# Seven block products in place of eight in the second feed-forward product of a streaming encoder step

## What is computed

```python
hn = rmsnorm(x, norm2_g[l]) * (1 + sc2) + sh2
x = x + gt2 * (jnp.square(jax.nn.relu(hn @ w_ff1[l])) @ w_ff2[l])
...
y = rmsnorm(x, final_norm_g) * (1 + scf) + shf
```

## Time and profile before

| what | value |
|---|---|
| median of three executions | 1235.04 us |
| the profiled execution, its own time | 1234.25 us |
| its span, first to last instruction | 1232.4 us |
| PE busy | 1208.6 us, 98% of the span |
| DVE, ACT, POOL busy | 722.8, 440.6 and 120.7 us |
| granted clock of PE, mean of the span | 0.994 |

### The profile page before, as it was taken

How to read it: one execution, slowest core, us unless ns; L and a number is a source line. 1 busy time by engine, 2 the same in 40 slices (tenths; PEclk the granted TensorE clock), 3 DMA queues, 4 the chain that set the end, 5 groups by cost and what they waited for, 6 DMA issues and landing times.

```text
span 1232.4 us, 25278 instructions
## 1 busy us (share of the span) xinstructions
PE 1208.6 (98%) x10327; PEld 1156.4 (94%) x10327; DVE 722.8 (59%) x1087; ACT 440.6 (36%) x768; POOL 120.7 (10%) x282
## 2 busy tenths in 40 slices
PE   6999999999999999999999999999999999999997
PEld 3899999989999999999999999969999999999997
DVE  5686776545565564544968995574643444444445
ACT  4584443123232222324343333363332332233254
POOL 4111112102002021021110001000300000000000
PEclk8999999999999999999999999999999999999999
DMA  9722323222222122135864567422422322222212
GB/s 328 243 79 77 86 72 93 62 53 70 62 69 79 51 71 58 40 108 157 240 202 127 164 214 282 147 61 77 135 86 85 86 86 82 85 80 79 87 54 77
DMA packets 181559, 135.32 MB, mean 110 GB/s; under 512 B 4554, under 2 KB 168876, under 8 KB 180184
## 3 DMA queue, kind: packets, MB, share of 16 engines
q1 hardware_dynamic: 174228, 105.36, 29.2%
q0 software_dynamic: 6976, 28.48, 6.9%
q10 hardware_dynamic: 260, 0.10, 0.0%
HBM read 128.02 MB, written 5.90 MB: 109 GB/s over the span
## 4 chain that ended last, share of the span: by engine, by line
PE 94%; DVE 3%; ACT 1%; DMA 1%; SPq 1%; issue 1%; POOL 0%; DVEq 0%; ACTq 0%
PE gp L625 17%; PE gp L626 16%; PE gp L627 16%; PE gp L630 12%; PE gp L629 12%; PE gp L618 9%; PE dp L865 2%; PE dp L875 1%; DMA ada_w<-in_ada_w 1%; PE dp L932 1%; PE dp L898 1%; PE dp L925 1%; PE dp L917 1%; PE dp L877 1%; PE dp L904 1%; PE dp L835 1%
## 5 line engine op out<-in xcount | busy, mean ns | idle before, releaser
L625 PE MATMUL gp<-a_pair,w_hi 128*128 128x384 f32 x832 | 290.6, 349 | 3.9 <-DVE w_lo L1518 2.3
L626 PE MATMUL gp<-a_pair,w_hi 128*128 128x384 f32 x832 | 280.5, 337 | 0.0
L627 PE MATMUL gp<-a_pair,w_hi 128*128 128x384 f32 x832 | 279.7, 336 | 0.0
L630 PE MATMUL gp<-a_pair,w_lo 128*128 128x288 f32 x832 | 245.5, 295 | 0.0
L629 PE MATMUL gp<-a_pair,w_lo 128*128 128x288 f32 x832 | 243.8, 293 | 0.0
L1518 DVE TENSOR_TENSOR w_lo<-w_raw,w_hi 128x1024 fp32r<-128x1024 f32 x160 | 197.9, 1237 | 54.9 <-ACT w_hi L1117 54.7
L1271 ACT ACTIVATE xp<-gp 128x576 f32<-128x576 f32 x113 | 73.6, 652 | 419.1 <-PE gp L630 391.6
L1530 DVE TENSOR_TENSOR xp<-xp,gp 128x288 f32<-128x288 f32 x95 | 43.0, 453 | 226.2 <-ACT xp L1271 225.7
L625 PEld LDWEIGHTS gp<-a_pair,w_hi 128*128 128x128 f32 x832 | 156.1, 188 | 15.8 <-issue 6.2
L1117 ACT ACTIVATE w_hi<-w_raw 128x1024 fp32r<-128x1024 f32 x160 | 168.5, 1053 | 0.0
L626 PEld LDWEIGHTS gp<-a_pair,w_hi 128*128 128x128 f32 x832 | 156.7, 188 | 0.2 <-issue 0.2
(11 more groups left out here) (333 smaller groups left out, 1709.7 us busy)
## 6 DMA issues: line engine op xcount, KB each, us to landing
w_raw<-in_w_in SPq DMA_DIRECT2D x72, 512.0 KB, 3.9
w_raw<-in_w_ff SPq DMA_DIRECT2D x64, 512.0 KB, 4.1
ada_half<-in_ada_w POOLq DMA_DIRECT2D x32, 512.0 KB, 4.7
ada_w<-in_ada_w SPq DMA_DIRECT2D x16, 512.0 KB, 9.9
w_raw<-in_w_a_out SPq DMA_DIRECT2D x8, 512.0 KB, 4.8
w_raw<-in_w_b_out SPq DMA_DIRECT2D x8, 512.0 KB, 4.6
w_raw<-in_w_o SPq DMA_DIRECT2D x8, 512.0 KB, 6.5
fin_vu<-in_final_ada_w POOLq DMA_DIRECT2D x4, 1024.0 KB, 18.5
```

Of the source, the lines that this page charges most:

```text
L625: T_.matmul(front, w_hi[:, b, k, :], hi[:, 0:CUT], start=first, stop=False)
L626: T_.matmul(front, w_hi[:, b, k, :], lo[:, 0:CUT], start=False, stop=last)
L627: T_.matmul(both.rearrange("p (e c) -> p e c", e=2)[:, :, REST // 2:HALF], w_hi[:, b, k, :], pair[:, :, k, CUT:T], start=first, stop=last)
L630: return T_.matmul(back[:, REST:REST + HALF], w_lo[:, b, k, :], hi[:, HALF:T], start=False, stop=last, skip_group_check=True)
```

## The change

In quarters 0, 1 and 2, `ff2` is done on pairs of output tiles. A pair is a product of 2 x 2 blocks: two output tiles, two halves of the quarter's 1024 rows, two halves of 288 tokens. Eight block products become seven, of sums and differences of blocks (the scheme that is known by Strassen's and Winograd's names). Quarter 3 keeps its eight tiles.

- A block product is 4 steps of 3 matmuls of 288 columns. PE does seven of them for a pair (`seven_products`), on sums that accumulate in three PSUM banks. ACT copies the running sum out after the products 0, 1, 2 and 6 (`snapshot`), and DVE adds the products 3, 4 and 5 to those copies (`z_add`). PE waits for a copy before it goes on adding to the same bank.
- DVE makes four sums of weight blocks for each pair (`op_sums`). Rounded parts come from ACT (`op_hi`, four instructions a pair), rests from DVE (`op_lo`, four a pair), and `op_ready` counts the rests. Those of a quarter's first pair are made during the last four hidden tiles.
- Each two hidden tiles become eight blocks of 288 tokens, four as they are and four differences (`f_sum`), each rounded and split (`f_hi`, `f_hi_late`, `f_lo`). Tiles t and t + 4 stand side by side, so the order of the hidden tiles is 0, 4, 1, 5, 2, 6, 3, 7.
- There is one set of blocks `fo` in place of two buffers, and the order is ff1(0), ff2(0), ff1(1), ff2(1), ff1(2), ff2(2), ff1(3), ff2(3).
- `z_tok`, `shift` and `final_b` move to the place of `a_pair`, so POOL loads `final_b` and `shift` only when the last hidden tile is done. `ff1` and `ff2` are written out in place of loops.

```diff
+PRODUCTS = ((4, R11), (5, T1), (6, T2), (0, R22), (1, T3), (2, R21), (3, T4))
+BANK_C, BANK_A = 1, 3
...
         pool.wait_ge(S["ada_used"], 3 * KT)
+        pool.wait_ge(S["tile_done"], ordinal(N_FF + 55) + 1)
         pool.dma_start(final_b[:, :], A["final_ada_b"][0:D].rearrange("(o d) -> o d", o=1).to_broadcast([P, D]))\
...
+        def seven_products(q, m):
...
+            for at, (slot, op) in enumerate(PRODUCTS):
+                pe.wait_ge(S["op_ready"], 4 * i + (1, 2, 2, 3, 3, 4, 4)[at])
...
+                elif at == 1:
+                    if m:
+                        pe.wait_ge(S["z_added"], 3 * i - 2)
+                elif at == 2:
+                    pe.wait_ge(S["snapped"], 4 * i + 1)
+                elif at == 3:
+                    pe.wait_ge(S["snapped"], 4 * i + 2)
...
+                for k in range(KH):
+                    if m == 0:
+                        pe.wait_ge(S["f_split"], 12 * q + 3 * k + (1 if op in (R11, T1) else 3 if op in (T3, T4) else 2))
+                    T_.matmul(out, hi[:, k, :], fo[:, 0, k, op, :], start=(opens and k == 0), stop=False,
+                              skip_group_check=not opens)
+                    T_.matmul(out, hi[:, k, :], fo[:, 1, k, op, :], start=False, stop=False, skip_group_check=not opens)
+                    last = T_.matmul(out, lo[:, k, :], fo[:, 0, k, op, :], start=False, stop=(k == KH - 1),
+                                     skip_group_check=not opens)
+                last.then_inc(S["part_done"], 1)
...
         for q in range(3):
-            group8(N_FF + 8 + 16 * q, a_pair)
+            for m in range(4):
+                seven_products(q, m)
...
+            products(n, 0, a_pair, summed=kept(n) + 1)
...
+        def ff1(q):
+            for t in range(KT):
+                n, b = N_FF + 16 * q + t, t % 2
+                evac(n, b, xp[:, b, 0:T], also="tmp_free", value=n - N_WA + 1)
+                if q == 0 and t == 0:
+                    act.wait_ge(S["ada_used"], 3 * KT)
+                if t < 6 or q == 3:
+                    w_next(n + 2)
+                f_hi(q, t)
+                if q < 3:
+                    if b:
+                        f_hi_late(q, t)
+                    if t >= 4:
+                        op_hi(q, 0, t - 4)
...
+        def ff2(q):
...
+                snapshot(i, 0, chain, xp[:, 0, 0:HALF])
+                if m < 3:
+                    op_hi(q, m + 1, 0)
+                act.wait_ge(S["tmp_free"], n - N_WA + 2)
+                snapshot(i, 1, more, xp[:, 1, HALF:T])
+                snapshot(i, 2, chain, xp[:, 0, HALF:T])
...
-        ff1(0, N_FF)
+        ff1(0)
         ada_rows(B2, mrow_l, 3 * KT, 3)
         for q in range(3):
-            ff1(q + 1, N_FF + 8 + 16 * q)
-            ff2(q, N_FF + 16 + 16 * q)
+            ff2(q)
+            ff1(q + 1)
...
+                elif b == 0:
+                    f_sum(T1, R12, R11, "tmp_free", squared).then_inc(S["f_raw"], 1)
+                    if t < 6:
+                        lo_split(n + 2, (n + 2) % 4)
+                    dve.wait_ge(S["f_hi_done"], 12 * q + 3 * u + 1)
+                    f_lo(q, t, R11, T1 + 1, 2)
...
+                    elif t == 6:
+                        op_lo(q, 0, 1)
+                        op_sums(q, 0, 1)
+                        op_sums(q, 0, 2)
+                        op_lo(q, 0, 2)
...
+                z_add(i, 5, alone, xp[:, 0, 0:HALF])
+                if m == 3:
+                    lo_split(n + 2, (n + 2) % 4)
+                dve.wait_ge(S["z_added"], 3 * i + 3)
+                add_residual(2 * m, 0).then_inc(S["tmp_free"], 1)
+                if m < 3:
+                    op_lo(q, m + 1, 1)
...
```

More of the change, by code:

```diff
@@ L53, with ordinal, pair_of, kept @@
 PLAIN = N_WA - N_TAIL
+KH = KT // 2
+R11, R12, T1, R21, R22, T2, T3, T4 = range(8)
+NOP = 8
+TILE_ORDER = (0, 4, 1, 5, 2, 6, 3, 7)
+PRODUCTS = ((4, R11), (5, T1), (6, T2), (0, R22), (1, T3), (2, R21), (3, T4))
+BANK_C, BANK_A = 1, 3
+def ordinal(n):
+    return n - 8 * min((n - N_FF) // 16, 3) if n >= N_FF else n
+def pair_of(q, m):
+    return 4 * q + m
+def kept(n):
+    return ordinal(n) - PLAIN
 RAW, SLOT = 4, 2
@@ L399, in _, with ff_load @@
         group8(N_WO, w_o)
[L400 to L404, removed]
+        def ff_load(n, w, col, row=0):
+            before = n - 4
+            q, r = divmod(before - N_FF, 16)
+            if before >= N_FF and r >= 8 and q < 3:
+                sp.wait_ge(S["op_ready"], 4 * (pair_of(q, (r - 8) // 2) + 1))
+            else:
+                sp.wait_ge(S["w_lo_done"], ordinal(before) + 1)
+            sp.dma_start(w_raw[:, n % 4, :, :], wt(w, col, row)).then_inc(raw_full[n % 4], 16)
+        for q in range(4):
+            for t in range(KT):
+                at = TILE_ORDER[t] if q < 3 else t
+                ff_load(N_FF + 16 * q + t, w_ff1, q * D + at * P)
+            for t in range(KT):
+                ff_load(N_FF + 16 * q + 8 + t, w_ff2, t * P, q * KT)
         for t in range(4):
@@ L627, in add_in @@
             T_.matmul(both.rearrange("p (e c) -> p e c", e=2)[:, :, REST // 2:HALF], w_hi[:, b, k, :],
-                      pair[:, :, k, CUT:T], start=first, stop=last)
+                      both_halves[:, :, CUT:T], start=first, stop=last)
             T_.matmul(front[:, 0:HALF], w_lo[:, b, k, :], hi[:, 0:HALF], start=False, stop=last, skip_group_check=True)
@@ L1087, in _ @@
         for n in range(N_ALL - KT, N_ALL - 1):
[L1088 removed]
+            products(n, n % 2, fo, "f_split", 36, summed=kept(n) + 1)
             f = n - N_ALL + KT - 1
@@ L1431, in _ @@
             modulated(1, 1, KT, f)
[L1433 to L1447, removed]
@@ new lines, in snapshot @@
+        def snapshot(i, at, bank, out):
+            act.wait_ge(S["part_done"], 7 * i + at + 1)
+            AC(out, bank, ACT.Copy).then_inc(S["snapped"], 1)
+        def ff2(q):
+            for m in range(4):
+                i, n = pair_of(q, m), N_FF + 16 * q + 8 + 2 * m
+                chain, more = gp[:, 2 * (m % 2), 0:HALF], gp[:, BANK_C, 0:HALF]
+                act.wait_ge(S["tmp_free"], n - N_WA + 1)
+                snapshot(i, 0, chain, xp[:, 0, 0:HALF])
[5 more added lines that the diff above has]
+                if m < 3:
+                    op_hi(q, m + 1, 1)
+                else:
+                    act.wait_ge(S["part_done"], 7 * i + 5)
+                    w_next(n + 2)
+                if m < 3:
+                    op_hi(q, m + 1, 2)
+                snapshot(i, 6, chain, xp[:, 1, 0:HALF])
+                if m < 3:
+                    op_hi(q, m + 1, 3)
+                else:
+                    w_next(n + 3)
@@ L1464, in _ @@
             if n + 2 < N_ALL:
-                free(n, n // 4, n % 4)
+                w_next(n + 2)
             if t == 0:
@@ L1992, in _ @@
         norm(rstd2, 1)
[L1994 to L2003 removed]
+        slot_lo = w_lo[:, :, :, :].rearrange("p b (h k) n -> p (b h) k n", h=2)
@@ new lines, in op_lo @@
+        def op_lo(q, m, which):
+            i, n = pair_of(q, m), N_FF + 16 * q + 8 + 2 * m
+            j = n % 4
+            dve.wait_ge(S["op_hi"], 4 * i + which + 1)
+            if which == 0:
+                out, full, hi = e_lo[:, 0], w_raw[:, j, 0:KH, :], e_hi[:, 0]
+            elif which == 1:
+                out, full, hi = e_lo[:, 1:3], e_sum[:, :, :, :], e_hi[:, 1:3]
+            elif which == 2:
+                out, full, hi = slot_lo[:, 0:2], w_sum[:, :, :, :], slot_hi[:, 0:2]
+            else:
+                out, full, hi = slot_lo[:, 2:4], w_raw[:, j:j + 2, KH:KT, :], slot_hi[:, 2:4]
+            TT(out, full, hi.bitcast(F32), ALU.subtract).then_inc(S["op_ready"], 1)
```

266 lines of the change are left out of this document (213 added, 53 removed).

## The result

The changed kernel takes 1246.05 us (median of 6 runs, 1245.24 to 1248.19) against 1234.75 before: 11.3 us slower, a ratio of 1.0092 [1.0081, 1.0103]. I had forecast 1238.8 and a range of 1232 to 1244. The sign was right and the size was not: the kernel is 7.3 us slower than I said.

What follows compares the result with a forecast made beforehand. PE, busy 98% of the span, bounds the kernel. Saving -16.7, stalls +12.5, modulation row +0.6, small terms +1.4, +0.45, +1.0, clock +4.5: +3.75 us on 1234.25, so 1238.0, as median 1238.8; range 1232 to 1244.

Steps and rivals of the forecast that it cites:

- The saving: ff2 pairs in quarters 0 to 2: 11.20 us in place of 12.59, 16.7 us saved for twelve pairs.
- No gap inside the quarters: Nine pairs after each quarter's first: DVE and ACT keep up with PE, no gaps; tightest margin 0.3 us before product 1.
- DVE becomes the bound: Rival, inside the quarters: slower DVE operations and waits make a pair 11.9 us, nine times 0.7 more, 1245 us; chance 0.10.
- the stalls are short: Rival, before product 2: slack in the chain, PE waits under 3 us, the clock stays, 1230.7 us; chance 0.10.
- The stalls: Where ff1 ends and ff2 begins, three quarters: PE waits 4.18 us before product 2 for ACT's copy, 12.5 in all.
- The clock at the stalls: Behind each of three waits before product 2 the clock falls to half: 1.5 us each, bounds 0 and 2.2, 4.5 together.
- (b): Third hidden tile of quarter 0: DVE's new difference of 288 delays the rest of the weights, 0.45 us more.
- (c): Output norm at the end: later loads delay the first scaled row, 1.0 us, bounds 0 and 2.5.
- (a): Where ff2 ends and ff1 begins: the next weights' rest is late on DVE, 0.45 us three times, 1.4.

Runs made afterwards that it cites:

- experiment 1: Changed kernel, but ACT no longer waits for POOL's two additions before its first scaled row at the output norm: 1240.5 us.
- experiment 2: Changed kernel, but in quarter 0's first hidden tile ACT rounds the next weights before waiting for the modulation products, and DVE takes their rest before the difference: 1242.81 us.
- experiment 3: Changed kernel plus 24 matmuls with unread results ahead of the wait before product 2, in the first pair of quarters 0 to 2: 1238.77 us.
- experiment 4: Changed kernel, but in the last hidden tile of quarters 0 to 2 ACT copies products 0 and 1 ahead of the rounding for weights: 1235.55 us.
- experiment 5: Experiment 4's kernel, with the third set of product weights for a quarter's first pair rounded after the last tile's read-out, its rest taken late on DVE: 1231.61 us.

## Why the prediction was right or wrong

- **The saving** was right: 11.16 us a pair against 11.20 worked out, 17.1 saved against 16.7. The price of a matmul in the earlier trace rows holds in the new products.
- **No gap inside the quarters** was right: nine pairs run without one, on a margin of 0.4 us where I had worked out 0.3 (in the second pair of quarter 0 the rest for product 1 ends at 886.92, the product starts at 887.34). "DVE becomes the bound" fell, and so did "the stalls are short".
- **The stalls** were right in place, cause and nearly in size: 4.34, 3.86 and 3.78 us against 4.18, and 4.8 with the modulation row in quarter 0. The two later ones are 0.3 to 0.4 shorter than the chain made them.
- **The clock at the stalls** fell, as forecast, but its price was mis-sized: "I take 1.5", with bounds of 0 and 2.2, where 2.5 was measured in the trace, 1.3 to 2.65 in those of experiments 1 and 2, and 2.4 in the mean by experiment 3. I took the upper bound from half of the 4.40 us that the start of the kernel showed at 0.50; here the clock stayed down through up to 5.4 us of work. One row gave one sample of that stretch, not its upper end. In the profiled execution this is 3.0 us of the 10.1 by which the table lies above my sum of 3.75; (b) is 2.2 of them, (c) 4.6, and 2.3 have no cause; the saving, the stalls' length and (a) came out 2.0 better.
- **Term (b)**, "a difference of 288 now stands between: 0.45", failed. I priced DVE's instruction and passed over ACT's new wait for `ada_used`, which the diff shows ahead of the rounding of the weights. That is 1.0 us of gap, and a fall of the clock that cost another 1.7. Experiment 2 gave back 3.2.
- **Term (c)**, "I take 1.0 for three loads at once in place of two; the bounds are 0 and 2.5", failed by most: 5.6 in the trace, 5.5 by experiment 1. The loads came 2.3 us later than the two of the earlier trace rows, the gap grew to 3.2, and the clock fell behind it. The landing took 6.9 to 7.2 us in all seven traces with the three loads, so that part is no accident; the fall is not in every execution (experiments 4 and 5). My bounds had a wait in them and no clock.
- Both (b) and (c) broke on one step: I had asked of the three large stalls whether they trip the clock and of the small waits not. The earlier trace rows gave me 1.48 us as a gap that leaves the clock at 1.00, and I read it as if every gap up to some 4 us did. Nothing in the trace spoke of gaps between 1.5 and 4 us, so each of the two had to have a fall in its bounds. With two more of up to 2.5 us my upper end of 1244 would have been 1249.

What stays open: why a gap of some 3 us trips the clock in some executions and not in others, and why the low clock then lasts longer in some; whether the gaps of 1.7 us in experiment 4 ever tripped it; why the three loads landed 2.3 us later than two had; and the 0.1 us a tile by which one quarter's hidden tiles are slower in some executions.

## What to carry to other kernels

A gap on a PE that was full costs its length and, where the clock falls, another 1.3 to 2.65 us at half clock. In the traces of this case the clock fell behind all nine stalls of 3.6 to 4.2 us, all five gaps of 2.4 and three of the five of 3.0 to 3.2, and behind none of the six of 1.4 to 1.7. Price each new wait with both, the small ones too, and fill a gap that can't go. Ahead of a saving in matmuls, lay out on each helper engine what stands in its list in front of the instruction that PE waits for, new waits included; here three edits to those lists and waits turned a loss of 0.9% into a gain of 0.9%.

## What the runs showed of the hardware that I had not expected

- The clock can fall after work has come back. Behind the gap of (b), PE is busy again at 828.36 and the clock is 1.00 for another microsecond before it drops (0.86 in 828 to 830, 0.50 in 830 to 832). At the stalls of this trace it fell during the gap; in experiment 2's first one it fell after it too (PE starts at 872.00, the clock is 1.00 from 872 to 873 and 0.51 from 873 to 876).
- The same gap can trip the clock in one execution and leave it alone in the next: behind (c)'s gap it fell in the traces of the changed kernel and of experiments 2 and 3 (3.16, 3.10 and 3.17 us), and stayed at 1.00 in those of experiments 4 and 5 (3.22 and 2.95 us). A single trace doesn't price such a wait.
- DVE slows beside POOL's additions. The rest of 1024 columns, 1.22 to 1.23 us elsewhere, took 2.34 while POOL added (1184.13 to 1189.81), and 2.1 to 2.4 in the same place of the six experiments' traces:

```profile
1185.27 2.34 DVE L1718 TENSOR_TENSOR w_lo<-w_raw,w_hi 128x1024 fp32r<-128x1024 f32 x1 [1.70 <-ACT w_hi L1229]
```

PE waited for the scaled row then, so it cost nothing here. The kernel before has it too, where I had not looked. DVE in that trace, beside POOL's additions of the earlier trace rows:

```profile
878.59 3.43 DVE L1518 TENSOR_TENSOR w_lo<-w_raw,w_hi 128x1024 fp32r<-128x1024 f32 x1
881.93 2.96 DVE L2002 TENSOR_TENSOR f_pair<-acc,f_pair 128x576 f32 x1
```

(The Trainium skill, SBUF — State Buffer, section "🔬 SBUF: two separate sides", says that VectorE and GpSimd share a pair of ports, which one of them holds for a whole instruction while the other waits. The longer durations point the same way; no run here takes the additions away.)
